# Opening loads on one queue, a bias table written once and read reversed, and the second block's output product in half-column pieces

## The reference

```
kv   = rmsnorm(mem) @ w_mem_kv                       # opening: 256 x 2048 @ 2048 x 1024
h    = rmsnorm(x) @ w_in                             # then u_ssm, queries, keys, values
y    = [neighbourhood attention, S5 state space, memory attention], each normed
x    = x + rmsnorm(y @ w_out)
x    = x + rmsnorm(square(relu(rmsnorm(x) @ w_ff1)) @ w_ff2)
# second block: four mixers of 512 columns
y    = [latent attention, forget-gate attention, sparse attention, window attention]
       # the last two add a bias  tbl[head, bucket(query - key)]  to the scores
x    = x + groupnorm(y) @ w_out_2
x    = x + square(relu(rmsnorm(x) @ w_up_2)) @ w_down_2
out  = rmsnorm(x)
```

## Time and profile before

| | |
|---|---|
| median of 3 runs | 2383.89 us (2381.69 to 2387.66) |
| the profiled execution | 2381.89 us |
| its span, first to last instruction | 2380.1 us |
| busy PE, DVE, ACT, POOL | 97%, 58%, 41%, 7% of the span |
| mean granted TensorE clock | 0.987 of full |

### The profile page before, as it was taken

The page is one execution under the profiler, slowest core; times in us unless marked ns, Lnnn a source line. Parts: engine busy times, 40 slices in busy tenths (PEclk is TensorE's granted clock), DMA queues, the critical chain, the costliest instruction groups (busy, mean ns, idle before and its releaser), DMA issues.

```text
span 2380.1 us, 31199 instructions
## 1 busy us (share of the span) xinstructions
PE 2300.5 (97%) x12622; PEld 1937.8 (81%) x12622; DVE 1370.6 (58%) x1483; ACT 980.1 (41%) x1290; POOL 166.7 (7%) x61
## 2 busy tenths in 40 slices
PE   7999999998999999999999999999999999999997
PEld 6887667787888888888888888787888888888886
DVE  5799846464554554444466478556545545444444
ACT  5212145343334344444444366535333444444443
POOL 0697400000000000000000000000000000000000
PEclk9999999999999999999999999999999999999999
DMA  8355334558656655565543533245566665555551
GB/s 304 114 141 142 114 100 166 177 132 223 193 181 189 183 187 195 193 245 192 190 146 115 198 107 93 100 153 164 174 192 188 192 191 181 194 194 194 194 194 71
DMA packets 151056, 404.24 MB, mean 170 GB/s; under 512 B 15168, under 2 KB 26688, under 8 KB 130368
## 3 DMA queue, kind: packets, MB, share of 16 engines
q1 hardware_dynamic: 135616, 385.51, 49.0%
q10 hardware_dynamic: 15360, 17.61, 3.4%
HBM read 396.80 MB, written 6.29 MB: 169 GB/s over the span
## 4 chain that ended last, share of the span: by engine, by line
PE 82%; DVE 8%; DMA 3%; ACT 3%; POOL 3%; issue 1%; ACTq 1%; SPq 0%; POOLq 0%; DVEq 0%
PE ps L657 18%; PE ps L695 11%; PE ps L697 11%; PE ps L696 11%; PE ps L658 9%; PE ps L564 4%; PE ps L580 2%; DVE w_low L1895 2%; DMA raw_weights<-in_w_ff 1%; PE ps L572 1%; DMA raw_weights<-in_w_mem_kv 1%; ACT w_high L1252 1%; PE ps L853 1%; PE ps L573 1%; PE ps L855 1%; PE ps L574 1%
## 5 line engine op out<-in xcount | busy, mean ns | idle before, releaser
L1895 DVE TENSOR_TENSOR w_low<-raw_weights,w_high 128x1024 fp32r<-128x1024 f32 (+1 forms) x628 | 738.4, 1218 | 801.8 <-ACT w_high L1252 801.7
L1252 ACT ACTIVATE w_high<-raw_weights 128x1024 fp32r<-128x1024 f32 (+1 forms) x628 | 628.7, 1049 | 846.9 <-PE ps L697 455.2
L657 PE MATMUL ps<-x_split,w_high 128*128 128x512 f32 x2048 | 724.1, 398 | 12.6 <-DVE w_low L1895 10.1
L658 PE MATMUL ps<-x_split,w_low 128*128 128x256 f32 x2048 | 576.5, 281 | 0.0
L657 PEld LDWEIGHTS ps<-x_split,w_high 128*128 128x128 f32 x2048 | 386.3, 189 | 105.8 <-DVE w_low L1895 10.3
L695 PE MATMUL ps<-w_high,x_split 128*128 128x512 f32 x1152 | 448.9, 390 | 3.1 <-DVE w_low L1895 3.1
L696 PE MATMUL ps<-w_low,x_split 128*128 128x512 f32 x1152 | 448.2, 389 | 0.0
L697 PE MATMUL ps<-w_high,x_split 128*128 128x512 f32 x1152 | 448.2, 389 | 0.0
L658 PEld LDWEIGHTS ps<-x_split,w_low 128*128 128x128 f32 x2048 | 389.2, 190 | 0.0
L695 PEld LDWEIGHTS ps<-w_high,x_split 128*128 128x128 f32 x1152 | 216.4, 188 | 48.8 <-DVE w_low L1895 4.0
L697 PEld LDWEIGHTS ps<-w_high,x_split 128*128 128x128 f32 x1152 | 216.3, 188 | 45.0
(11 more groups left out here) (260 smaller groups left out, 2165.6 us busy)
## 6 DMA issues: line engine op xcount, KB each, us to landing
raw_weights<-in_w_ff SPq DMA_DIRECT2D x128, 1024.0 KB, 5.2
raw_weights<-in_w_up SPq DMA_DIRECT2D x64, 1024.0 KB, 5.2
raw_weights<-in_w_down SPq DMA_DIRECT2D x64, 1024.0 KB, 4.9
raw_weights<-in_w_in SPq DMA_DIRECT2D x62, 1024.0 KB, 5.6
raw_weights<-in_w_out SPq DMA_DIRECT2D x32, 1024.0 KB, 4.9
raw_weights<-in_w_mem_kv SPq DMA_DIRECT2D x8, 1024.0 KB, 15.4
t_table<-region ACTq DMA_DIRECT2D x1, 4096.0 KB, 45.8
region<-t_table ACTq DMA_DIRECT2D x1, 3072.0 KB, 17.8
```

What stands on the lines that cost most here:

```text
L657: nc.tensor.matmul(o, wh[:, q, w], xs[:, kt], start=(kt == 0), stop=False, skip_group_check=True)
L658: last = nc.tensor.matmul(o[:, 0:S], wl[:, q, w], xh[:, kt], start=False, stop=(kt == KT - 1), skip_group_check=True)
L1252: nc.scalar.activation(split_slot(wh_t, k)[:, r], ring_slot(n)[:, r], ACT.Copy).then_inc(rounded, 1)
L1895: V.tensor_tensor(split_slot(wl_t, k)[:, r], ring_slot(n)[:, r], split_slot(wh_t, k)[:, r].bitcast(f32), ALU.subtract).then_inc(split_read ...
```

## The change

Three edits. (1) SP issues all opening loads in order of use: a piece of `memT`, a weight slot, and so on, then x, then the state-space parameters between the slots of "memv". ACT keeps only `gains` and `ident`, and runs one small activation at the start. `group3` waits for each half of a split slot by itself, and "u" starts when the first four tiles of x are out. (2) The table is written to HBM once (16 rows of 2 KB) instead of 128 times; it is stored reversed, read back with a shift of p, and the duos read it with a negative step. (3) The end of the second block's mixers gets the form of `wout1`: the latent norm moves to "fva", the other norms and the last three duo steps go between half-column pieces of the output product.

```diff
-        t5_dram = nc.dram_tensor("t5_table", (2 * HEADS, P, 2 * S), f32, kind="Internal")
+        t5_dram = nc.dram_tensor("t5_table", (2 * HEADS, 2 * S), f32, kind="Internal")
...
-            return [heads_of(t5, i, j)[:, :, P * (TT - 1 - t):P * (TT - 1 - t) + P * (t + 1)] for t in range(TT)]
+            both = heads_of(t5, i, j)
+            return [both[:, :, 384 - P * (TT - 1 - t) - P * (t + 1):384 - P * (TT - 1 - t)][:, :, ::-1] for t in range(TT)]
...
+            for c in range(4):
+                sp.dma_start(mem_f[:, 4 * c:4 * c + 4], A["memT"][:, 4 * c:4 * c + 4]).then_inc(mem_loaded[c], 16)
+                load(rows(w, 0, 512, SK * c))
+            sp.dma_start(xres[:, :, :], A["xT"]).then_inc(x_loaded, 16)
+            load(rows(w, 512, 512, 0))
+            sp.dma_start(rinv[:, S:S + 96], A["ssm_p"]).then_inc(ssm_loaded, 16)
+            sp.dma_start(bd, A["ssm_b"]).then_inc(ssm_loaded, 16)
+            load(rows(w, 512, 512, SK))
+            sp.dma_start(cd, A["ssm_c"]).then_inc(ssm_loaded, 16)
+            sp.dma_start(iota, A["iota"]).then_inc(ssm_loaded, 16)
...
+                        if q % (sk // 2) == 0:
+                            pe.wait_ge(split_ready, 2 * k + 1 + q // (sk // 2))
...
-            pe.wait_ge(dve_done, at("x", "out"))
-            group("u", xn)
+            group("u", xn, ready="x")
...
+                    if g == "fva" and kt == 6:
+                        pe.wait_ge(act_done, at("evac", "fk"))
+                        norm("latent", xo[:, 0:4], [(0, 4)], bank=2)
...
-            for p in range(TAIL0, ND + 3):
-                duo_step(p)
-            pe.wait_ge(dve_done, at("window", "sumread"))
-            norm("group", xo[:, 12:16], [(0, 4)], bank=1)
-            down("wout2", WOUT_ITERS, "group")
+                pe.wait_ge(dve_done, at("group", "out", 0))
+                left_half(k, 0, 0, True, [(act_done, at("evac", "fva")), (act_done, at("evac", "fvb"))])
+                duo_step(TAIL0)
+                pe.wait_ge(dve_done, at("scaled2", ND - 1))
+                norm("window", xo[:, 4:12], [(0, 4), (4, 4)], bank=4)
+                left_half(k, 1, 1, False)
+                duo_step(TAIL0 + 1)
+                left_half(k + 1, 0, 2, False)
+                duo_step(TAIL0 + 2)
+                left_half(k + 1, 1, 3, False)
+                right_halves(k + 2, 0, True, [scores_read, nothing, forget_sums, forget_read])
+                right_halves(k + 3, 2, False)
+                full_rows("wout2", "group")
...
-                act.dma_start(t5_dram.ap(), t5tab[0:2 * HEADS, :].unsqueeze(1).to_broadcast([2 * HEADS, P, 2 * S])).then_inc(t5_out, 16)
+                act.dma_start(t5_dram.ap(), t5tab[0:2 * HEADS, :]).then_inc(t5_out, 16)
...
+            act.wait_ge(dve_done, at("ones"))
+            m.did(nc.scalar.activation(st[:, 36:37], onec, ACT.Copy, scale=onec))
...
+            evac_rows("fvb", *homes["fvb"])
+            rounds("wout2", 1)
+            duo_back(TAIL0)
+            rounds("wout2", 2)
+            duo_back(TAIL0 + 1)
+            root("window", 2, 1)
+            duo_back(TAIL0 + 2)
...
+            moment("window", 1, 512, ps[:, 4, 0:S])
+            moment("window", 2, 512, ps[:, 4, S:2 * S])
+            lows("wout2", 2)
+            part_full("group", "wout2", 1, 1, "window")
+            moment("group", 3, 512, ps[:, 7, 0:S])
+            lows("wout2", 3)
+            part_low("group", "wout2", 1)
+            part_full("group", "wout2", 2, 2, "window")
+            part_low("group", "wout2", 2)
+            lows("wout2", 4)
```

More of the change, by code:

```diff
@@ L286, in half_rows_ps @@
         def half_rows_ps(product, t, right):
-            if product != "wout1":
+            if product not in TILES_OF:
                 return rows_ps(t)[:, RIGHT if right else LEFT]
@@ L488, in down @@
                 state["n"] = n0 + BODY * iters
-            group(A["w_mem_kv"], 0)
-            group(A["w_mem_kv"], 512)
+            w = A["w_mem_kv"]
+            for c in range(4):
[8 more added lines that the diff above has]
+            sp.dma_start(iota, A["iota"]).then_inc(ssm_loaded, 16)
+            for c in range(2, 4):
+                load(rows(w, 512, 512, SK * c))
             w = A["w_in"]
@@ L521, in _ @@
                     load(rows(w, c0, 256, 8 * j, 8))
-            out_rows("wout2", A["w_out_2"])
+            for c0 in (0, D // 2):
+                for a in (0, 2):
+                    load(rows(A["w_out_2"], c0, D // 2, a, 2))
+            for kt in (*range(8, 16), *range(4, 8)):
+                load(A["w_out_2"][P * kt:P * kt + P, :])
             up("ff1_2", A["w_up_2"])
@@ L589, in tall3, with group @@
                 return last
-            def group(name, x, form="wide", width=512, between=None):
+            def group(name, x, form="wide", width=512, between=None, ready=None):
                 acc_free(name)
                 for j in range(KT // SK):
+                    if ready is not None:
+                        pe.wait_ge(dve_done, at(ready, "out", j))
                     n, w = take()
@@ L843, in glu @@
                 book["acc", "glu"] = m.n
[L845 to L860, removed]
-                pe.wait_ge(dve_done, at("outn", "out", 0))
-                pe.wait_ge(dve_done, at("ssmn", "sumread"))
-                pe.wait_ge(dve_done, at("memn", "sumread"))
-                for j in range(2):
-                    for n in range(2):
[L867 to L896, removed]
@@ new lines, in out_product, with left_half @@
+            def out_product(pos, t, c, wh, wl, first):
+                o = ps[:, 4 * (c // 2) + 2 * t + c % 2, :]
+                h, l = (x[:, pos, P * t:P * t + P] for x in (xh, xl))
+                nc.tensor.matmul(o, h, wh, start=first, stop=False, skip_group_check=True)
+                nc.tensor.matmul(o, h, wl, start=False, stop=False, skip_group_check=True)
+                return nc.tensor.matmul(o, l, wh, start=False, stop=True, skip_group_check=True)
+            def left_half(k, n, pos, first, free=None, at_turn=None):
+                pe.wait_ge(split_ready, 2 * k + n + 1)
+                wh, wl = (split_slot(x, k)[:, HALF * n:HALF * n + HALF] for x in (wh_t, wl_t))
+                for t in range(TT):
+                    if free is not None:
+                        pe.wait_ge(*free[t])
+                    for c in range(2):
+                        last = out_product(pos, t, c, wh[:, 512 * c:512 * c + 512], wl[:, 512 * c:512 * c + 512], first)
+                last.then_inc(*((half_done, 1) if n == 0 else (split_used, 1)))
@@ new lines, in right_halves @@
+            def right_halves(k, pos, first, before=()):
+                pe.wait_ge(split_ready, 2 * k + 2)
+                for q in range(4):
+                    t, c = q // 2, q % 2
+                    if before:
+                        before[q]()
+                    for n in range(2):
+                        wh, wl = (split_slot(x, k)[:, HALF * n + 512 * c:HALF * n + 512 * c + 512] for x in (wh_t, wl_t))
+                        last = out_product(pos + n, t, 2 + c, wh, wl, first and n == 0)
+                    if q == 0:
+                        last.then_inc(half_done, 1)
+                last.then_inc(split_used, 1)
```

121 lines of the change are left out of this document (66 added, 55 removed).

## The result

| | before | after |
|---|---|---|
| median of 4 runs each | 2382.79 us (2379.81 to 2387.66) | 2368.94 us (2364.32 to 2372.27) |
| ratio, 95% interval | | 0.9945 (0.9928 to 0.9962) |
| profiled execution, its span | 2381.9, 2380.1 us | 2372.3, 2370.3 us |

The account below looks back on a forecast made before the run. PE, busy 97% of the span, was taken as the bound, so only its gaps and slow clock could be won. Opening -7.8, table -8.6, mixers' end -4.0, copy +0.15 gave -20.2 us: 2363.6 us, range 2355 to 2371.

Parts of the forecast that it names:

- Start of PE: Opening: weight 0 lands at 7.2 us, first matmul 2.3 us later at 9.5, gaining 5.2 us.
- the waits of 1.2, 0.8 and 0.6: Opening: PE's waits in "memk", at the last slot of "memv" and before "u" go; with the start's 5.2, 7.8 us.
- The side sum with the slower memory rate: Opening: at 358 GB/s weight 0 would land 0.4 us later and the gain be 7.4 us.
- Is it kept?: State-space stage: DVE's constants move about 7 us, "u" covers the difference, ACT's "k0" wait passes the 7.8 us on.
- rival A: Opening given back by late weights or the state-space stage's own pace: worth 3 us, total 2368.5 us; chance 0.10.
- Bias table: Around 550 us: the small write removes 7.1 us idle and 1.5 us of slow clock, 8.6 us together.
- rivals C and D: Table: C, slow read back, 2372.3 us, chance 0.04; D, negative step lengthens DVE reads, 2397.7 at k = 3.5, chance 0.03.
- End of the mixers: Second block's output product: 8.6 us of idle and slow clock go, 4.7 us of new waits come, gain 4.0 us.
- three forecast waits: Output product: PE waits for DVE's `w_low` 1.9 us at slot 3, 2.0 at slot 4, 0.8 at slot 5.
- one of my own signs of being wrong: Output product: the forecast is wrong if the clock, expected at full, falls there.
- rival B: Mixers' end only trades waits, about 2 us gaps slow the clock: worth 0 to 1 us, total 2367.2; chance 0.12.
- Sum: Whole kernel: -7.8 - 8.6 - 4.0 + 0.15 = -20.2 us.

Follow-up runs that it names:

- b1: `w1` with `mem_high` waiting for `gains` alone, `na_loads()` ahead of `evac("k0")`, and the first `bu` two steps later: median 2352.36 us, ratio 0.9871.
- o1: The kernel before with only the opening edit (loads and waits): median 2379.87 us, ratio 0.9985.
- n3: The changed kernel without the mixers' end edit, POOL's neighbourhood-bias mask delayed until after the last scan: median 2360.08 us, ratio 0.9913.
- f1: `w1` with the two matmuls of every second 512/256-column pair exchanged: median 2351.41 us, ratio 0.9874.
- t1: The kernel before with only the bias table edit: median 2373.44 us, ratio 0.9970.
- m1: The kernel before with only the edit to the mixers' end: median 2380.14 us, ratio 1.0002.
- g1: `f1` without the opening edit: median 2357.70 us, ratio 0.9888.
- o2: The kernel before with the opening edit, and POOL's neighbourhood-bias mask delayed until after the last scan: median 2367.27 us, ratio 0.9936.
- c1: The kernel before with only POOL's neighbourhood-bias mask delayed until after the last scan: median 2372.82 us, ratio 0.9963.
- g2: `n3` with the two matmuls of every second pair exchanged: median 2360.01 us, ratio 0.9898.
- w1: The changed kernel with POOL's mask delayed until after the last scan and another DVE and ACT order in `wout2`: median 2353.75 us, ratio 0.9881.

## Why the prediction was right in part

**Start of PE: 9.5 forecast, 10.70 measured.** Weight 0 landed at 7.8 us (7.9 in `b1`), not 7.2; ACT started on it at 8.25, because it waited for `ident` first; and from the rounding to the first matmul it was 2.45 us, not 2.3. A further 0.8 us I had left out: PE's first matmuls start 0.213 us apart and later ones 0.12, and that first stretch was 27 matmuls (10.70 to 16.4) where before had 18 (14.71 to 18.5); what sets that pace the traces do not show. Everything else in the opening went as written: ACT waits for PE, not for loads, and PE has no gap until 94 us. With the waits of 1.2, 0.8 and 0.6 gone the lead at "u" is 6.4 us (6.2 on the mean of the five traces with the old opening), where I had 7.8. (The side sum with the slower memory rate comes to 0.5 us and not 0.4; nothing hangs on it.)

**Is it kept? This step failed in part, between "u" and the first `bu`.** I had written that DVE's state-space constants move by about 7 us, a little less than PE, and that "u" covers the difference. They moved by 4.7 us, PE by 6.4, and "u" did not cover that. By the starts PE leads by 4.6 us from 35 to 62 us, and DVE, which works from PE's sums there, by as much; the last two waits that went, at the last slot of "memv" and ahead of "u", gave PE 1.0 and 0.8 us more and DVE nothing. ACT makes the first chunk's tables behind the constants, and only then copies out what the first `bu` multiplies. The start of the tables and PE's wait for that copy (L1506, L1549), before and then after:

```profile
92.74 1.26 ACT L1467 ACTIVATE region<-ps,small_stats 128x512 f32<-128x512 f32 x2 [19.99 <-DVE region L1758]
...
PE ps L773 <- ACT region L1506: 0.2, 1, 0.2
```

```profile
88.03 1.26 ACT L1510 ACTIVATE region<-ps,small_stats 128x512 f32<-128x512 f32 x2 [19.98 <-DVE region L1803]
...
PE ps L781 <- ACT region L1549: 0.9, 1, 0.9
```

That wait takes 0.7 us of the lead. Behind it, at 98 us, PE's clock fell in the changed kernel's profile (1.2 instead of 2.4 GHz for a part of two windows that show 0.92 and 0.91; matmuls 0.43 us apart instead of 0.21), which took 1.5 more. Of the eight traces that have this gap, four show this (changed, `o1`, `n3`, `f1`). At one and the same matmul near 156 us the five traces with the old opening agree within 0.4 us; those with the new one are 3.5 to 5.1 us ahead of their mean where the clock fell, and 6.1 to 7.2 where it did not: 5.3 in the mean of all eight. In `b1`, whose first `bu` comes two steps later, gap and low clock are both absent, and it is 6.4 us ahead.

The rest of the path is as I had argued: what PE has left is passed on where ACT waits for "k0",

```profile
162.91 1.02 ACT L1318 ACTIVATE region<-ps 128x1024 f32<-128x1024 f32 x1 [5.26 <-PE ps L569]
```

4.2 us earlier than before, and the scans end 4.7 us earlier. Against `t1` and `m1` the kernels with the new opening, changed and `o1`, are 4.0 us ahead at "k0" and on, and 4.0 us ahead at "next group". So the opening is worth 5.3 us by eight traces, 3.6 (0.2 to 7.1) by the timing of the edit alone, and 6.3 to 6.4 by the medians of `g1` and `f1` and the timings of `o2` and `c1`. These agree within their intervals; 7.8 was too much.

This lies near the 3 us of rival A, whose sum of 2368.5 is beside the median of 2368.9, but that is luck: neither were the loads late, nor does the stage keep its own pace behind "k0". Only its constants, ahead of the first `bu`, moved less than PE. The wait for the scans, 3.0 us in the waits of before, I had not read at all. It took nothing from the forecast; it was 8.4 us that the change left lying.

**Bias table: 8.6 forecast.** Shift 8.7 us, timing 7.1 (3.8 to 10.7). The idle, the clock, the read back and the negative step were all as written; rivals C and D fell.

**End of the mixers: 4.0 forecast.** Shift 3.1 us (12.9 to 16.0), 3.5 by `g2`. One pair of traces would not carry that: from 1469 us to the full rows, seven traces with the old end took 102.1 to 105.6 us and the three with the new one 99.7 to 101.4; the means differ by 3.1. Two of the three forecast waits came near their sizes, 1.75 and 1.87 us where I had 1.9 and 2.0; the third, 0.8, did not. But the clock, which I had at full, was 0.83 for one window, one of my own signs of being wrong and rival B in small: that ate what the missing third wait gave. `w1` shows that these waits were not the price of the form: slot 3's remainder only stood behind a moment that had to wait for PE.

**Sum.** With 5.3 for the opening, 8.7 and 3.1 the change would be worth 17.1, just inside the measured 9.1 to 17.2. So 3.1 of the missing 7.1 us (20.2 against 13.1) have a cause, 2.5 of them in the opening; the other 4.0 are at the edge of the interval, and no run explains them. The spans of the profiled executions differ by 9.8 us alone, but after had the longer rate in both loops and before in `ff1_1` only: 15.7 at equal rates of `ff1_2`. That the median fell inside a range 16 us wide with a sum 7 us too large is in part luck.

## What to carry to other kernels

A shift won early is kept only if every chain that the bounding engine meets behind the change moves by as much: write down by how much each releaser moves, and take the difference off before calling it covered. Do not read the loss from one pair of traces. Here a wait grew from 3.0 to 4.7 us between them and looked like the thief, and it was 4.7 in two kernels without the edit; what had differed was a stretch of low clock in one execution of before. Work on GpSimd that nobody waits for is not free when VectorE works beside it; place it where VectorE does not carry the path, here 8.8 us for one added wait. Before a few us are looked for in medians, find out what makes the runs of one kernel differ, for a difference can also be read place by place from matmul to matmul.

## What was not expected of the hardware

- One and the same loop of matmuls (512 and 256 columns in turn) runs at 346.7 or at 353.3 ns a pair at a granted clock of 1.00, chosen at a restart after a wait and kept for up to 300 us; with every second pair exchanged it ran at 349.0 in both loops of three kernels.
- A pair of scans of 128x1024 took 4.47 us beside an idle POOL, 5.19 or 6.12 beside POOL's 128x1024 operations, and 13.03 when POOL had started an operation of 128x4096 (9.85 us) just before. Three times it ended within 0.15 us of POOL's end plus the scans' own time.
- The same gap of 1.3 us at about 94 us was followed by the lower clock in four of eight traces, so a gap of this size can cost nothing or some 2 us more. At 185 to 193 us the lower clock followed gaps of 1.1, 1.9, 2.5 and 3.7 us (before, `g1`, `g2`, `o2`), and did not follow four others of 1.2 to 1.3.
- fp32 reads with a negative step from SBUF: 693 and 437 ns, the same as forward.
